# Band attention: the probabilities are divided by their sums on VectorE ahead of the transposes, in place of a spread of the inverse sums

## The reference, cut to what matters

```python
sc = jnp.einsum('bqhd,bkhd->bhqk', q_c, k_c, preferred_element_type=jnp.float32) * scale + bias
sc = jnp.where(valid[None, None, None, :], sc, -1e30)
p = jax.nn.softmax(sc, axis=-1).astype(v.dtype)
return jnp.einsum('bhqk,bkhd->bqhd', p, v_c)
```

## Time and profile before

| | us |
|---|---|
| median of 3 runs | 2596.62 |
| lowest, highest | 2594.49, 2596.85 |
| profiled execution, its own time | 2594.16 |
| its span in the profile | 2592.4 |
| band attention, first matmul to last write | 1399.08 to 1515.03 |

### The profile page before, as it was taken

One profiled execution on the slowest core, in us unless ns is written; L12 is line 12 of the kernel. 1 busy time (PEld: TensorE's weight loads), 2 busy tenths in 40 slices (PEclk: granted clock), 3 DMA queues, 4 the chain that ended last, 5 costly groups with the idle time before them and its releaser, 6 DMA issues. The chain is left out here.

```text
span 2592.4 us, 28506 instructions
## 1 busy us (share of the span) xinstructions
PE 2414.8 (93%) x11168; PEld 1829.9 (71%) x11168; DVE 1580.5 (61%) x1700; ACT 1064.0 (41%) x1281; POOL 411.2 (16%) x284
## 2 busy tenths in 40 slices
PE   7999988949999999975999999998969999999998
PEld 6776554836666666655776778887858888887787
DVE  5552665357999999968212652223589998874444
ACT  4221103226777777755213641112344344433322
POOL 3110301011222222210300210000032333210000
PEclk9999998969999999997999999999989999999999
DMA  5121032269999999976310011113212222226343
GB/s 160 41 67 53 17 103 96 82 275 332 380 375 385 378 363 378 375 263 229 115 49 17 2 32 46 49 49 150 74 49 81 90 82 90 79 81 227 122 159 138
DMA packets 192965, 397.27 MB, mean 153 GB/s; under 512 B 17270, under 2 KB 120694, under 8 KB 176456
## 3 DMA queue, kind: packets, MB, share of 16 engines
q1 hardware_dynamic: 183624, 378.76, 41.2%
q0 software_dynamic: 9216, 16.80, 2.1%
HBM read 357.75 MB, written 47.18 MB: 156 GB/s over the span
## 5 line engine op out<-in xcount | busy, mean ns | idle before, releaser
L1398 DVE TENSOR_TENSOR expert_rest<-expert_raw,expert_high 128x2048 fp32r<-128x2048 f32 x135 | 306.1, 2290 | 43.7 <-ACT expert_high L1392 41.7
L1392 ACT ACTIVATE expert_high<-expert_raw 128x2048 fp32r<-128x2048 f32 x135 | 258.0, 1913 | 24.4 <-PE expert_up_ps L143 8.5
L141 PE MATMUL up_ps<-blocks_high,up_operand_high 128*128 128x512 f32 x616 | 241.5, 392 | 15.0 <-DVE plain_blocks_rest L3013 11.7
L143 PE MATMUL up_ps<-blocks_high,up_operand_rest 128*128 128x512 f32 x616 | 240.7, 391 | 0.0
L1805 POOL DMA_INDIRECT expert_rows<-y_rows,out_ids x32 | 84.5, 2639 | 425.2 <-DVE y_rows L1759 425.2
L141 PE MATMUL down_ps<-w_down_high,prod_high 128*128 128x512 f32 x352 | 138.2, 393 | 8.1 <-DVE w_down_rest L185 8.1
L141 PEld LDWEIGHTS up_ps<-blocks_high,up_operand_high 128*128 128x128 f32 x616 | 116.3, 189 | 41.0 <-issue 16.8
L3230 DVE TENSOR_TENSOR up_operand_rest<-res,up_operand_high 128x512 fp32r<-128x512 f32 x154 | 143.1, 940 | 3.0 <-ACT up_operand_high L3186 3.0
L1398 DVE TENSOR_TENSOR expert_rest<-res,expert_high 128x2048 fp32r<-128x2048 f32 x57 | 129.6, 2290 | 15.0 <-ACT expert_high L1392 14.4
L142 PE MATMUL down_ps<-w_down_rest,prod_high 128*128 128x512 f32 x352 | 137.7, 391 | 0.0
L142 PE MATMUL up_ps<-plain_blocks_rest,up_operand_high 128*128 128x512 f32 x352 | 137.6, 391 | 0.0
(11 more groups left out here) (432 smaller groups left out, 5944.1 us busy)
## 6 DMA issues: line engine op xcount, KB each, us to landing
expert_raw<-in_w_down_dram SPq DMA_DIRECT2D x46, 1024.0 KB, 19.1
expert_raw<-in_w_up_dram SPq DMA_DIRECT2D x45, 1024.0 KB, 19.4
expert_raw<-in_w_gate_dram SPq DMA_DIRECT2D x44, 1024.0 KB, 17.4
res<-in_w_up_dram SPq DMA_DIRECT2D x88, 256.0 KB, 3.9
res<-in_w_down_dram SPq DMA_DIRECT2D x44, 512.0 KB, 4.1
res<-in_w_gate_dram SPq DMA_DIRECT2D x20, 1024.0 KB, 22.0
res<-in_w_in_dram SPq DMA_DIRECT2D x38, 512.0 KB, 4.4
res<-in_w_up_dram SPq DMA_DIRECT2D x19, 1024.0 KB, 20.2
```

The costliest lines, as they stand in the source:

```text
L141: nc.tensor.matmul(out, w_high, x_high, start=start, stop=False)
L143: return nc.tensor.matmul(out, w_rest, x_high, start=False, stop=stop)
L1392: self.nc.scalar.activation(self.high_part[:, n % SPLIT_SLOTS, :], self.raw[n % RAW_SLOTS], ACT.Copy) \
L1398: self.nc.vector.tensor_tensor(self.rest_part[:, s, :], self.raw[n % RAW_SLOTS], self.high_part[:, s, :].bitcast(F32), ALU.subtract).then_ ...
```

## The change

The product of the attention output with the spread inverse sums goes, and with it all that made the spread: GpSimd's block, the matmul at L2533, and the copy at L2601. In its place VectorE, after scored(n), waits for each head's exponential, takes the reciprocal of that head's sum and multiplies the exponentials in `score` by it, in place. The transposes of a head wait for that product (`prob_done`) and no longer for the exponential. The attention output is then copied from PSUM to `attT` as it is, and that copy stands in VectorE's order ahead of the scored of the third item after it (`leave(n - 3)`), where the output product of item n - 2 stood behind the scored of item n.

```diff
-        spread = sb("inv_spread", [P, 2, 2, HEAD])
-        scale = sb("inv_across", [P, 2, P])
...
                     if j == 0:
-                        pe.wait_ge(exp_done, 2 * n + h + 1)
+                        pe.wait_ge(prob_done, 2 * n + h + 1)
...
-                        nc.tensor.matmul(ps_o[HEAD * h:HEAD * (h + 1), 0:P],
-                                         m.v[:, i + 1 - nk + j, head:head + HEAD], probT[:, n % 2, h * nk + j, :],
-                                         start=(j == 0), stop=(j == nk - 1))
-                pe.wait_ge(spread_done, n + 1)
-                nc.tensor.matmul(ps_o[:, P:2 * P], spread[:, n % 2, :, :].rearrange("p h d -> p (h d)"), m.ident[:],
-                                 start=True, stop=True).then_inc(pv_mm, 1)
+                        last = nc.tensor.matmul(ps_o[HEAD * h:HEAD * (h + 1), 0:P],
+                                                m.v[:, i + 1 - nk + j, head:head + HEAD], probT[:, n % 2, h * nk + j, :],
+                                                start=(j == 0), stop=(j == nk - 1))
+                last.then_inc(pv_mm, 1)
...
-        @block.gpsimd
-        def _(pool):
-            for n in range(N):
-                pool.wait_ge(inv_done, n + 1)
-                if n >= 2:
-                    pool.wait_ge(pv_mm, n - 1)
-                for h in range(2):
-                    last = nc.gpsimd.tensor_scalar(spread[:, n % 2, h, :], m.ones[:, 0:HEAD], inv[:, n, h:h + 1], None, ALU.mult)
-                last.then_inc(spread_done, 1)
-
         @block.vector
         def _(dve):
+            def scale_probs(n):
+                width = key_tiles(ITEMS[n][0]) * P
+                for h in range(2):
+                    dve.wait_ge(exp_done, 2 * n + h + 1)
+                    nc.vector.reciprocal(inv[:, n, h:h + 1], total[:, n, h:h + 1]).then_inc(inv_done, 1)
+                    dve.wait_ge(inv_done, 2 * n + h + 1)
+                    nc.vector.tensor_scalar(score[:, n % R, h, 0:width], score[:, n % R, h, 0:width], inv[:, n, h:h + 1],
+                                            None, ALU.mult).then_inc(prob_done, 1)
+
+            def leave(n):
+                i, c = ITEMS[n]
+                dve.wait_ge(pv_mm, n + 1)
+                nc.vector.tensor_copy(m.attT[:, c, i * P:(i + 1) * P], ps_o[:, 0:P]).then_inc(attT_done, 1)
+
             dve.wait_ge(m.masked, 2)
             for n in range(N + 2):
+                if n >= 3:
+                    leave(n - 3)
                 if n < N:
...
-                if 1 <= n <= N:
-                    dve.wait_ge(exp_done, 2 * n)
-                    nc.vector.reciprocal(inv[:, n - 1, :], total[:, n - 1, :]).then_inc(inv_done, 1)
-                if n >= 2:
-                    i, c = ITEMS[n - 2]
-                    dve.wait_ge(pv_mm, n - 1)
-                    nc.vector.tensor_copy(scale[:, n % 2, :], ps_o[:, P:2 * P]).then_inc(scale_done, 1)
-                    dve.wait_ge(scale_done, n - 1)
-                    nc.vector.tensor_tensor(m.attT[:, c, i * P:(i + 1) * P], ps_o[:, 0:P], scale[:, n % 2, :],
-                                            ALU.mult).then_inc(attT_done, 1)
+                if n < N:
+                    scale_probs(n)
+            leave(N - 1)
```

More of the change, by code:

```diff
@@ L2465, in band_attention @@
         inv_done = sem("inv_done")
-        spread_done = sem("spread_done")
-        scale_done = sem("inv_across_done")
+        prob_done = sem("prob_scaled")
         pv_mm = sem("pv_mm")
```

## The result

The changed kernel takes 2604.15 us in the median of 7 runs (2602.14 to 2605.39), the kernel before 2595.33 (2594.49 to 2596.85): 8.8 us more, a ratio of 1.0032 with a 95% interval of 1.0022 to 1.0042, which is 5.7 to 10.9 us. The profiled execution has a span of 2600.1 us against 2592.4. Its stage of band attention runs from the first scored at 1401.79 to the end of the last output copy at 1523.63, 121.84 us where it was 113.28. That is 8.56 us; the first matmul of the next stage is late by as much (1526.29 against 1517.70), the first one of the output projection by 8.0, the last of the kernel by 7.7.

The account below looks back on a forecast made before the run. TensorE's order of work was taken to bound the stage; after the change a ring through VectorE and ScalarE, 4.51 us against 4.18. The parts summed to +8.9 us, giving 2605.0 us, range 2599 to 2613.

Parts of the forecast that it names:

- TensorE sets the pace: Band attention before the change: TensorE's order of work sets the five-tile round, 4.18 us, 3.76 without the spread matmul.
- The multiply costs 0.55 us at 640 elements: VectorE's new multiply of score by a per-row scalar: 0.55 us at 640, 0.49, 0.42, 0.35 and 0.29 at smaller widths.
- both rivals about it: Score multiply at 0.39: +4, 2600, 11 in 100; one element a time in place: +15, 2611, 8 in 100.
- the row at 1024 elements: Another stage's SBUF to SBUF multiply with a scalar per row, 0.75 us, from which the new multiply's cost was estimated.
- The ring: Scored, first exponential, two copies, second exponential, reciprocal, multiply, output copy, next scored: 4.51 us against 4.18 with five tiles.
- TensorE's idle time: Five-tile rounds of the changed kernel: TensorE ends up idle 0.75 us a round.
- busy below 90%: Sign expected in the changed trace: TensorE busy below 90% of the band attention stage at clock 1.00.
- Fewer tiles: Steps between items with four, three, two and one key tiles: 3.84, 3.18, 2.7 and 2.1 us.
- The drain and the last steps: End of band attention: three one-tile steps 6.65 against 5.63, +1.0; drain some 3.8 against 5.36, -1.5 us.
- the one on the clock: Band attention: TensorE's gaps of 0.3 to 0.5 us a round leave its granted clock at 1.00.
- the 7 of the rival: TensorE's gaps cost it its 2.4 GHz: three or four slow rounds are +7, in all +16, 2612; 7 in 100.
- the gain: Rival: TensorE keeps the pace and the change gives back 0.42 us an item, -13.4, 2583; 5 in 100.

Follow-up runs that it names:

- the best version: Changed kernel with both exponentials before the copies, extra matmuls at two and one tiles, output copy in VectorE's gap only from three tiles: 2586.28 us, ratio 0.9963.

## Why the prediction was right

It was right in sign, size and mechanism: +8.9 forecast, +8.8 measured; 2605.0 against 2604.15. That the two agree to 0.1 us is luck: the interval is 5.7 to 10.9.

- **TensorE sets the pace, its removed matmul is worth 13.4 us.** Shown: -13.0 with the removal alone, and a round of 3.77 us against 3.76.
- **The multiply costs 0.55 us at 640 elements.** Measured 0.554, in place, and 0.486, 0.420, 0.354 and 0.286 at the smaller widths. That closes both rivals about it, and the row at 1024 elements was the right source. By the cycle table of the Trainium skill (VectorE: DVE Perf Modes, section on the TRN2 errata) the estimate was 0.39; the trace doesn't agree, and the section itself says that this row of its table comes out too low.
- **The ring.** Its terms were 1.07, 1.56, 0.98, 0.20, 0.48 and 0.22; they are 1.04, 1.57, 0.95, 0.20, 0.46 and 0.20, 4.43 in place of 4.51. No term is off by more than 0.03, but the errors have mostly one sign and add up to 0.08. Over 13 steps that is 1.0 us, the whole error of the five-tile part (58.6 against 57.58), and a like share went wrong with four and three tiles. That the ring is the cause with five tiles is shown by five kernels: it loses what is taken from it (multiplies, copies, output copy) and ignores what is added beside it (first multiply doubled).
- **TensorE's idle time** was put at 0.75 us a round. The step is 0.66 over the round of 3.77, and the trace has 0.42 idle. The sign "busy below 90%" holds for the whole stage (108.40 of 125 us, 87%), not for the five-tile stretch (47.07 of 52, 90.5%).
- **Fewer tiles.** 3.84, 3.18, 2.7 and 2.1 were forecast; 3.74, 3.13, 2.69 and 2.24 to 2.40 came. With two tiles the way through the transposes and the one copy is shown by the timeline and by the 2.47 with this copy behind the exponentials. With three that way is as long as VectorE's own, which the prediction didn't see.
- **The drain and the last steps** were mis-sized, +1.0 and -1.5 forecast, +1.4 and -0.6 measured. The step that failed is the one on the clock: I took it to hold wherever TensorE had short gaps, from a stretch with 3.43 us busy in 5. It held through all five-tile items, as said, but it went to 0.50 in the one-tile items, and so the whole drain ran at the low clock, where the kernel before still had 0.92 in 1511 to 1514 us. With the clock kept, 2.10 and 4.00 stand where 2.1 and 3.8 were forecast. A drop of the clock inside the stage was named as a sign of being wrong, and it came: it cost some 1.1 us (121.84 against 120.72), not the 7 of the rival, because it fell only with the last items. The Trainium skill, TensorE: Matmul & The Clock Gate, Part 1, ties the fall to idleness; the trace agrees with the five-tile items at 1.00, and in the one-tile items the idleness was in waits of 0.64 us at most.
- **The range and the rivals.** The change as made could not have the gain (TensorE keeps the pace), and the reason given was right: not VectorE's load, but the ring, here through ScalarE's copies. With those two copies out of it the step is 3.80, and most of the 13.4 us can be had after all: 9.2 in the best version.

The errors of the table nearly cancel (-1.7 in the items with five to three tiles, +1.3 in the last ones and the drain), so the sum of +8.9 is closer to the stage's +8.56 than its terms deserve. The 0.9 us between the stage's 8.56 and the span's 7.7 went in later stages, 0.6 of it in the next one; where there was not tried.

## What to carry to other kernels

When work moves to an engine with room, don't ask whether the engine has room, but whether the work lies on the way round: list what each engine waits for in one round, add the ring up from starts in the timeline, and compare it with the round of the busiest engine. Work beside the ring is free up to the gap, work in it costs its full time, and the cheapest cure may be to reorder a third engine's queue, here ScalarE's copies, which had been free as long as nobody waited for the second exponential. A gap measured at one size is not there at a smaller one: the first multiply doubled, the output copy moved and the extra matmuls were all dearer with two tiles than the gap with five had promised.

## What I had not expected of the hardware

TensorE's granted clock fell in a stretch without any long pause: in 1510 to 1513 us it was busy 2.27 of 3.00 us at 1.00, and in the 3 us behind 2.36 at 0.67, down to 0.50 (1.2 GHz). Its longest waits in 1508 to 1514 us were 0.43, 0.64 and 0.58 us. In the kernel with the second multiply doubled TensorE was busy for 42.19 of the 52 us of the five-tile stretch, and the clock was 1.00 throughout. Three small matmuls on constants in each round with two tiles or one kept it at 1.00 to the end.
